# A two-layer hybrid decoder: order of the r-k product, the stacks and the first inverse level in the mixer stage

## The reference, cut to what matters

```python
# latent attention: projections up, norms, rotary turns, causal attention
q = (rms_norm(q_a, q_a_gain) @ w_qb).reshape(B, S, MLA_HEADS, MLA_QK_DIM)
kv = (rms_norm(kv_a, kv_a_gain) @ w_kvb).reshape(B, S, MLA_HEADS, MLA_NOPE + MLA_V)
...
# RWKV-7: a linear recurrence over time, per head of 64
def step(state, inp):
    r_t, w_t, k_t, v_t, kk_t, a_t = inp
    sa = jnp.einsum('bhvk,bhk->bhv', state, -kk_t)
    state = (state * w_t[:, :, None, :]
             + sa[..., :, None] * (kk_t * a_t)[..., None, :]
             + v_t[..., :, None] * k_t[..., None, :])
    return state, jnp.einsum('bhvk,bhk->bhv', state, r_t)
...
bonus = (jnp.sum(r * k * r_k, axis=-1, keepdims=True) * v).reshape(B, S, RW_WIDTH)
```

## Time and profile before

| | |
|---|---|
| median of 3 runs (range) | 2366.62 us (2366.38 to 2368.61) |
| the profiled execution | 2367.02 us, its span 2365.2 us |
| PE busy | 2326.6 us, 98% |
| DVE busy | 1341.4 us, 57% |
| ACT busy | 1082.8 us, 46% |
| POOL busy | 64.3 us, 3% |
| chain that ended last | PE 94%, DVE 5%, issue 1% |
| TensorE's granted clock | 9 in each of 40 slices (in tenths) |

### The profile page before, as it was taken

How to read it: one execution, slowest core, us unless ns; L and a number is a source line. 1 busy time by engine, 2 the same in 40 slices (tenths; PEclk the granted TensorE clock), 3 DMA queues, 4 the chain that set the end, 5 groups by cost and what they waited for, 6 DMA issues and landing times.

```text
span 2365.2 us, 34149 instructions
## 1 busy us (share of the span) xinstructions
PE 2326.6 (98%) x13908; PEld 1929.4 (82%) x13908; DVE 1341.4 (57%) x1369; ACT 1082.8 (46%) x1287; POOL 64.3 (3%) x67
## 2 busy tenths in 40 slices
PE   7999989999999999999999999999999999999999
PEld 6888678888888888888888886888888888888887
DVE  5696576644555444445556857675454554454454
ACT  5554654444443344444445546444444433444433
POOL 1000110000000000000000002100000000000000
PEclk9999999999999999999999999999999999999999
DMA  8453304655555555555454533055555555555553
GB/s 314 165 183 119 132 3 178 205 203 189 184 194 187 191 194 194 193 180 195 179 194 151 193 113 106 21 182 191 185 189 195 181 192 196 196 187 187 194 185 136
DMA packets 60179, 411.27 MB, mean 174 GB/s; under 512 B 6688, under 2 KB 6720, under 8 KB 13472
## 3 DMA queue, kind: packets, MB, share of 16 engines
q1 hardware_dynamic: 58624, 401.63, 47.2%
q0 software_dynamic: 1440, 7.97, 1.0%
HBM read 407.48 MB, written 2.10 MB: 173 GB/s over the span
## 4 chain that ended last, share of the span: by engine, by line
PE 94%; DVE 5%; issue 1%; ACT 0%; DMA 0%; DVEq 0%; POOL 0%; ACTq 0%; POOLq 0%
PE psum L1459 28%; PE psum L1461 28%; PE psum L1460 28%; PE psum L1620 2%; PE psum L1868 1%; PE psum L1715 1%; PE psum L1955 1%; PE psum L1470 1%; PE psum L1521 1%; DVE arena L1202 1%; DMA gain<-gains_dram 0%; DVE arena L1272 0%; DVE small L1186 0%; DVE arena L1183 0%; PE psum L1696 0%
## 5 line engine op out<-in xcount | busy, mean ns | idle before, releaser
L870 DVE TENSOR_TENSOR w_lo<-raw,w_hi 128x1024 fp32r<-128x1024 f32 (+2 forms) x752 | 901.6, 1205 | 841.6 <-ACT w_hi L453 834.7
L453 ACT ACTIVATE w_hi<-raw 128x1024 fp32r<-128x1024 f32 (+2 forms) x752 | 782.0, 1044 | 1099.2 <-PE psum L1461 1086.7
L1459 PE MATMUL psum<-w_hi,hT_hi 128*128 128x512 f32 (+2 forms) x2128 | 821.8, 386 | 3.8 <-DVE w_lo L870 2.5
L1461 PE MATMUL psum<-w_hi,hT_lo 128*128 128x512 f32 (+2 forms) x2128 | 816.6, 384 | 0.0
L1460 PE MATMUL psum<-w_lo,hT_hi 128*128 128x512 f32 (+2 forms) x2128 | 816.4, 384 | 0.0
L1459 PEld LDWEIGHTS psum<-w_hi,hT_hi 128*128 128x128 f32 x2128 | 399.8, 188 | 82.6 <-issue 2.5
L1461 PEld LDWEIGHTS psum<-w_hi,hT_lo 128*128 128x128 f32 x2128 | 399.8, 188 | 78.2
L1460 PEld LDWEIGHTS psum<-w_lo,hT_hi 128*128 128x128 f32 x2128 | 400.0, 188 | 76.5
L1459 PE MATMUL psum<-w_hi,act_hi 128*128 128x512 f32 x880 | 343.6, 390 | 0.0
L1461 PE MATMUL psum<-w_hi,act_lo 128*128 128x512 f32 x880 | 342.5, 389 | 0.0
L1460 PE MATMUL psum<-w_lo,act_hi 128*128 128x512 f32 x880 | 342.4, 389 | 0.0
(11 more groups left out here) (312 smaller groups left out, 1213.0 us busy)
## 6 DMA issues: line engine op xcount, KB each, us to landing
raw<-stream_dram SPq DMA_DIRECT2D x360, 1024.0 KB, 4.8
raw<-stream_dram SPq DMA_DIRECT2D x16, 512.0 KB, 3.5
raw<-stream_dram SPq DMA_DIRECT2D x8, 768.0 KB, 4.5
raw<-stream_dram SPq DMA_DIRECT2D x8, 640.0 KB, 3.8
gain<-gains_dram POOLq DMA_DIRECT2D x3, 1024.0 KB, 6.9
x<-x_in_dram SPq DMA_DIRECT2D x4, 512.0 KB, 8.8
out_dram<-x SPq DMA_DIRECT2D x4, 512.0 KB, 5.5
lor<-lora_dram POOLq DMA_DIRECT2D x2, 832.0 KB, 12.0
```

The costliest lines, as they stand in the source:

```text
L453: nc.scalar.activation(w_hi[:, q % HALF_RING, 0:2 * w], raw[:, j % 4, hf * 2 * w:(hf + 1) * 2 * w], ACT.Copy).then_inc(hi_done, 1)
L870: tt(w_lo[:, q % HALF_RING, 0:2 * w], raw[:, j % 4, hf * 2 * w:(hf + 1) * 2 * w], w_hi[:, q % HALF_RING, 0:2 * w].bitcast(F32), SUB).then_ ...
L1459: mm(o, a_hi, w_hi[:, r, cols], start=(k == 0), stop=False)
L1461: last = mm(o, a_lo, w_hi[:, r, cols], start=False, stop=(k == n_k - 1))
```

## The change

It has these parts, in both layers unless said otherwise.

- PE's order: before, `up(5)` stood ahead of the r-k product. Now the r-k product, and in layer 1 the stack of the values, stand ahead of `up(5)`. In layer 0 the value stack waits for `rw_shifted` instead of `rw_v_ready`, which only layer 1 raises now.
- ACT's order: `q_out(1)`, which waits for the r-k product, stands ahead of `up_out(5)`.
- PE's order: `stack(rw_a, 0)`, named the key stack in the change's title, stands behind both `r_turn`s.
- DVE: the 2 x 2 blocks of the inverse are formed from M in PSUM rather than from `mab`; the mask of level 0 is applied by DVE, from PSUM too, after the transposed copy and a wait for `mla_rope_done`; `mab` is written after that. POOL applies the masks of levels 1 to 4 only. `level_x(0)` waits for `rw_m_ready` before it overwrites the banks.

```diff
--- before.py
+++ after.py
@@ -429,9 +429,8 @@
 
 
                 pool.wait_ge(S("rw_m_ready"), 4 * l + 1)
-                for k in range(len(RW_LEVELS)):
-                    if k:
-                        pool.wait_ge(S("rw_gt_mm"), 10 * l + 2 * k)
+                for k in range(1, len(RW_LEVELS)):
+                    pool.wait_ge(S("rw_gt_mm"), 10 * l + 2 * k)
                     tt(rw_level, mab, lev_lo[:, k, :].unsqueeze(1).broadcast_to([P, JC, RC]), ALU.mult).then_inc(
                         S("rw_level_ready"), 1)
 
@@ -728,8 +727,8 @@
                 act.wait_ge(S("rw_exp"), 3 * l + 2)
                 nc.scalar.activation(rw_e_b, rw_b, ACT.Exp, scale=C0).then_inc(S("rw_exp"), 1)
                 nc.scalar.activation(srw[:, 48:64], srw[:, 32:48], ACT.Exp, scale=-C0).then_inc(S("rw_half_decay"), 1)
+                q_out(1)
                 up_out(5)
-                q_out(1)
                 k_std(0)
                 stacked(0, v_st, 0)
                 up_out(6)
@@ -1246,7 +1245,7 @@
                     dve.wait_ge(S("rw_vmix_ready"), 4 * l)
                     v(stt(rw_v, rw_bonus, 1.0, rw_v, SUB, MUL))
                     v(tt(rw_v, v_first[:, :, :], rw_v, SUB))
-                dve.sem_inc(S("rw_v_ready"), 1)
+                    dve.sem_inc(S("rw_v_ready"), 1)
                 v(tt(rw_a, rw_a, rw_kk, MUL))
                 q_norm()
                 dve.wait_ge(S("rw_exp"), 3 * l + 1)
@@ -1288,12 +1287,16 @@
                             settle()
                             dve.sem_inc(S("rw_xt"), 1)
 
-                product(1, mab, 2, "strict_lo")
-                v(tt(inv, mab, over(C("pair_lo"), JC, RC), MUL))
+                dve.wait_ge(S("rw_m_mm"), 4 * l + 1)
+                v(tt(inv, bank(2, 2).rearrange("p (n t) -> p n t", n=JC), over(C("pair_lo"), JC, RC), MUL))
                 vs(stt(inv, inv, -1.0, over(idst, JC, RC), MUL, ADD), "rw_x", 10 * l + 1)
                 vs(turn_blocks(inv_t, inv), "rw_xt", 12 * l + 1)
                 dve.sem_inc(S("rw_x"), 1)
                 dve.sem_inc(S("rw_xt"), 1)
+                dve.wait_ge(S("mla_rope_done"), ev)
+                v(tt(rw_level, bank(2, 2).rearrange("p (n t) -> p n t", n=JC), over(lev_lo[:, 0, :], JC, RC), MUL))
+                dve.sem_inc(S("rw_level_ready"), 1)
+                product(1, mab, 2, "strict_lo")
                 k_norm(1)
                 dve.wait_ge(S("rw_half_decay"), ev)
                 hd = srw[:, 48:64].rearrange("p (j c) -> p j c", j=4)
@@ -1759,6 +1762,8 @@
                         ns = range(8 * hf, 8 * hf + 8)
                         pe.wait_ge(S("rw_gt_ready"), 10 * l + 2 * k + hf + 1)
                         pe.wait_ge(S("rw_x"), 10 * l + 2 * k + hf + 1)
+                        if k == 0:
+                            pe.wait_ge(S("rw_m_ready"), 4 * l + 1)
                         if not last:
                             both_heads(2 + hf, ns, tile_of(inv), tile_of(g_t), RC).then_inc(S("rw_dinv_mm"), 1)
                         else:
@@ -1806,9 +1811,8 @@
                 q_turn(1)
                 pe.wait_ge(S("rw_kk_normed"), ev)
                 if l == 0:
-                    pe.wait_ge(S("rw_v_ready"), ev)
+                    pe.wait_ge(S("rw_shifted"), 4 * l + 3)
                     stack(rw_v, 0)
-                up(5)
                 pe.wait_ge(S("rw_rk"), ev)
                 pe.wait_ge(S("rkb_ready"), 4 * ev)
                 if l:
@@ -1817,17 +1821,18 @@
                     last = mm(bank(2, 2)[:, j * SEQ:(j + 1) * SEQ], rkb[:, j, :], rw_tmp[:, j, :], start=True, stop=True)
                 last.then_inc(S("rw_bonus_mm"), 1)
                 if l:
-                    pe.wait_ge(S("rw_v_ready"), ev)
+                    pe.wait_ge(S("rw_v_ready"), l)
                     stack(rw_v, 0)
+                up(5)
                 up(6)
                 up(7)
                 k_turn(0)
                 pe.wait_ge(S("rw_b_done"), ev)
                 product(rw_kk, rw_a, 2)
+                r_turn(range(4))
+                r_turn([4])
                 pe.wait_ge(S("rw_stacked"), 3 * l + 1)
                 stack(rw_a, 0)
-                r_turn(range(4))
-                r_turn([4])
                 attend(0)
                 pe.wait_ge(S("rw_stacked"), 3 * l + 2)
                 level_g(0)
```

## The result

The changed kernel takes 2371.15 us (median of 16 runs, 2369.49 to 2374.76) where the kernel before takes 2367.26 (16 runs beside them, 2366.04 to 2368.65): a ratio of 1.0017, 95% interval 1.0010 to 1.0023. The forecast was 2369.9 and no change by the bound of 0.2%; the measurement is +3.9 us, slower by less than that bound, though its interval (from 1.0010 up) leaves out a change of nothing.

A forecast was written before the change was run, and what follows sets the result against it. VectorE's chain from M's masking to the last probabilities was taken as the bound. Layer 0 (-1.4 + 1.36 + 0.9 = +0.9) and layer 1 (+0.1 + 1.36 + 0.9 = +2.4) gave +3.3 on 2366.62: 2369.9 us, range 2363.5 to 2372.7.

The forecast's parts named there:

- What bounds: Mixer stage, both layers: VectorE's chain from the masking of M to the last probabilities ends last.
- rival A: Mixer stages: the matrix engine's removed waits count whole, 8.0 us over both layers, giving 2358.7 us; chance 0.07.
- The reading of the blocks: VectorE's chain: instructions with two SBUF inputs wait until GpSimd's is over; four blocks cost 5.13 us per layer.
- Part 1: Order of matrix engine and ScalarE: M's masking starts 1.4 us earlier in layer 0, 0.1 us later in layer 1.
- Part 2: Key stack behind the rotary turns: removes 1.22 us waits ahead of the first attention block, 0 for VectorE's chain.
- Part 3: Inverse from PSUM, level 0 mask on VectorE: +1.36 us of VectorE per layer, bounds 1.23 and 1.7.
- Part 4: GpSimd's blocks move to decay product (2.0 us) and first probabilities (1.8): +0.8 to +0.9 us per layer.
- Rival B: GpSimd's blocks don't move to the new places; layers -2.1 and -0.6 us, total 2363.9 us; chance 0.24, partial case included.
- Rival C: GpSimd's rotary products and VectorE's products for b block once more per layer, b 1.1 us later: 2372.1 us; chance 0.13.
- The sum: Both mixer stages: layer 0 +0.9 us, layer 1 +2.4 us, together +3.3 us, median 2369.9 us.

The follow-up runs named there:

- the order alone: Kernel before with only the matrix engine's and ScalarE's new order (r-k product, value stack, query copy earlier); masks, inverse, key stack as before: 2365.66 us, ratio 0.9992.
- the kernel with the wait filled: Changed kernel plus 64 small unused matmuls in the wait ahead of the second turn of probabilities, both layers: 2371.74 us, ratio 1.0018 against the kernel before.
- the inverse alone: Kernel before with only the inverse begun from PSUM and the level 0 mask on VectorE; matrix engine's order as before: 2370.13 us, ratio 1.0012.
- the first group: The four kernels (order, inverse, decay product ahead, GpSimd gated) timed with 11 runs each beside 33 of the kernel before, at 2367.82 us.
- the change with both repairs: Changed kernel with the decay product ahead of the work on M and GpSimd's level 2 and 3 masks held behind probabilities: 2364.84 us, ratio 0.9986 against before.
- the decay product ahead: Changed kernel with VectorE's 12-column decay product moved ahead of the work on M: 2366.19 us, ratio 0.9995 against the kernel before.
- GpSimd gated: Changed kernel with GpSimd's level 2 mask also waiting for the first probabilities and its level 3 mask for the last: 2366.25 us, ratio 0.9994 against before.
- key stack alone: Kernel before with only the second stack moved behind the rotary turns: 2367.87 us, ratio 1.0000.
- both repairs without the inverse: Change's order and stack, decay product ahead, level 2 and 3 masks gated, but inverse from masked M, all masks on GpSimd: 2366.59 us, ratio 0.9997 against before.

## Why the prediction was right, point by point

- **What bounds.** Right: VectorE's chain. The forecast of a wait "grown from 1.30 to 4 us or so over the two turns before it" is 2.73 + 1.30 = 4.03 in layer 0 and 2.75 + 0.68 in layer 1; rival A, the waits counted whole, is refuted by the order alone, which took away the 1.45 and 1.26 us of layer 0 and the 0.77 of layer 1 and gained 1.3 us in all, and by the change itself. The places were right to a tenth: with T the end of the level 0 mask (299.02), the decay product came at T+3.01 (3.05 forecast) and the level 2 mask at T+12.91 (12.9).
- **The reading of the blocks.** "Each blocked row ends just after GpSimd's does" isn't so for all four: in the earlier trace rows L1293 ends at 298.79, 1.08 us behind GpSimd's 297.71, and L1202 at 324.99, 0.55 behind. A blocked instruction takes the rest of GpSimd's and then its own time: 2.18 + 1.23 less 0.15 for L1293, 2.07 + 0.17 less 0.14 for the decay product of the change. The short ones only look as if they ended with it. The prices weren't hurt, since they were taken as the excess over the unblocked duration.
- **Part 1**, -1.4 and +0.1: -1.39 and +0.29 by the masking's start; alone, -1.22 and -0.06. In layer 1 the key sums started 1.85 us later in their stage (1.6 forecast), and nearly all of it came back in two products that met less of GpSimd's rotary ones (L1255 takes 1.53 where it took 2.14, L1261 1.22 for 2.18).
- **Part 2**, 0: right for the change and for layer 0; wrong as a general statement, since alone it cost 1.0 us in layer 1. The step that failed is "on the matrix engine's side alone": the wait came back as 2.59 us ahead of level 0's products, the clock fell there, and GpSimd's next mask came 1.3 us later, onto a small product.
- **Part 3**, +1.36: +1.29 and +0.93. In layer 1 a pause of 0.67 us that stood behind the transposed copy went too, which the term didn't take in. On PSUM against SBUF: the masking from PSUM takes 1.22 us (L1291), the one from SBUF beside it 1.22 (L1292). The Trainium skill (Perfetto Trace Analysis, Optimizing Scalar/DVE Operations) gives PSUM the larger overhead; no difference shows at this size, and the measurement decides.
- **Part 4**, +0.8 to +0.9 for each layer: +0.58 and +1.19. Both new blocks came as named, 1.93 and 1.95 us, forecast as 2.0 and 1.8. Level 3's, taken as unchanged, moved to the last probabilities and lost 0.33 in layer 0, by the luck of the slow clock, as the kernel with the wait filled shows; in layer 1 the small products gave back 0.65 only, since one of them had not been blocked before. The rule of the Trainium skill (SBUF — State Buffer, Who interferes with whom) that two SBUF inputs against a GpSimd reader are enough held for 12 columns: 0.17 became 2.10. The upper bound of this term, +1.7, should be +1.8 by its own blocks (2.4 + 2.4 + 2.16 less 5.13).
- **Rival B**, blocks that don't move: didn't come in the change, but did in layer 0 of the inverse alone (-0.67), which shows how near it was: GpSimd missed the decay product by 0.4 us there, and the first probabilities too (1.03).
- **Rival C**, b a further 1.1 us late: the block that C named came (b's product L1260 takes 2.17 us for 1.22), but the key norm ahead of it started 1.19 us earlier and took 0.14 less, and b ends at 47.53 us of the stage for 47.92 before. In layer 1 b came 1.2 us later, as part 1 had it (1.1). No loss beyond that.
- **The sum**: +3.3 forecast, +2.7 by the stages, +3.9 by the medians with an interval of some +2.4 to +5.4. The two agree within that, and that the sum came so near is in part luck: by the stages part 3 was 0.4 too high in layer 1 and part 4 0.3 too high in layer 0 and 0.3 too low in layer 1. The 1.2 us between stages and medians aren't settled. The executions with a lower mean granted clock were the longer ones: of the 33 of the kernel before beside the first group, 26 with 1.000 average 2367.2 us and 7 with 0.998 or 0.999 average 2370.6; of the change, ten with 0.998 average 2370.4 and three with 0.996 average 2374.3. None of the change's 16 had more than 0.998. So spells at the low clock that the profiled execution doesn't show may be part of the +3.9; no run separates them.

## What to carry to other kernels

Where GpSimd and VectorE share work, cost a reordering by where GpSimd's long instructions will *start*: their start follows another engine's waits, and any VectorE instruction with two SBUF inputs that comes then, even of 12 columns, pays for all of the rest of it. Put such tiny products ahead of the region where GpSimd can be asked, and gate GpSimd until VectorE is past the larger ones; these two small edits turned a change that lost 3.9 us into one that gains 2. An early wait of the busiest engine that is hidden behind another engine's chain isn't time to be won, and may be what keeps two other engines apart. When a block is priced, the blocked instruction pays the rest of the other engine's and then its own time.

## What the runs showed of the hardware

**The matrix engine's clock fell behind short waits.** The change's view by stretches (start and end, length, busy time of PE, PEld, DVE, ACT, POOL, then the granted clock, DMA share and GB/s):

```profile
322.00:324.00 2.00, 1.59 (x30) 1.62 (x32) 1.90 (x4) 2.00 (x9) 0.00 (x0) 0.50 0.00 0
324.00:326.00 2.00, 2.00 (x50) 1.94 (x48) 1.79 (x6) 1.84 (x4) 0.17 (x1) 0.69 0.00 0
...
1500.00:1502.00 2.00, 2.00 (x44) 2.00 (x42) 1.75 (x8) 1.49 (x4) 0.15 (x1) 0.50 0.00 0
```

Behind the waits of 2.73 and 2.75 us the granted clock is 0.50, 1.2 GHz of 2.4: from about 321.9 to 325.2 us in layer 0 and from 1496 to 1502.8 in layer 1. In the kernel before, the order alone and the change with both repairs it stayed full through both stages. The longer busy time of the page is this and the start-up: 2.25 us ahead of the first stage, 0.86 in it, 2.26 in the second, sum 5.4.

The length of the wait doesn't foretell it. Spells came behind waits of 2.75, 2.74 (layer 1 of the inverse alone), 2.73, 2.59 and 2.20 us. None came behind the 2.21 us of layer 1 in the kernel whose layer 0 had one behind 2.20. In layer 1 of the kernel with the wait filled one came behind 0.73 and 1.30. And two came just behind the measured stages, at waits of only 1.07 and 1.06 us in the recurrence, where the eight other kernels have the same wait and no spell in either layer; with the decay product ahead, in layer 0:

```profile
346.01 0.93 PE L1873 MATMUL psum<-gain,arena 64*64 64x64 f32 x16 [1.07 <-DVEq L1288]
346.67 1.12 PE L1873 MATMUL psum<-arena 64*64 64x64 f32 x16
```

and with GpSimd gated in layer 1. With the full clock these 16 take 0.68.

What a spell costs depends on what else is late there. Behind level 1 in the change it was nothing that shows, since VectorE's chain covered it. Ahead of level 0, where GpSimd's next mask follows the slow products, it came with 1.0 us (key stack alone, layer 1) and 1.9 us (both repairs without the inverse, layer 0). In the recurrence nothing covered it: the way from there to the next stage took 1064.88 us for 1063.76, and in the gated kernel the way to the end 844.3 for 842.9: 1.1 and 1.4 us that the stages of the table leave out.

**The start-up differs by about 2 us between executions**, as the 0.63 and 0.40 us products above show, in code that is the same in all ten kernels. It is of the size of what this change does, and is a reason to read stages rather than spans.
